# One transformer kernel: the order of half products, exponentials and copies around its attentions

## The reference, cut to what matters

```python
logits = jnp.einsum('bqhd,bkhd->bhqk', qi, k) * scale      # plus a bias
logits = jnp.where(valid, logits, NEG)
p = jax.nn.softmax(logits, axis=-1)
out = jnp.einsum('bhqk,bkhd->bqhd', p, v)
...
wts = jax.nn.softmax(jnp.stack(lses), axis=0)               # dilated: three patterns joined
mixed = jnp.concatenate([o_a, o_b], axis=-1) @ w_out
```

## Time and profile before

| | |
|---|---|
| median of three runs | 1631.53 us (1631.42 to 1632.28) |
| the profiled execution | 1632.0 us, span 1630.3 us, mean granted clock 0.998 |
| PE busy | 1599.5 us, 98% of the span, 9172 matmuls |
| DVE, ACT, POOL busy | 1123.3 us (69%), 942.7 us (58%), 123.8 us (8%) |
| HBM | 281.81 MB read, 174 GB/s over the span |
| costliest lines | L1121 and L1122 (feed-forward, 27% and 13% of the chain that ended last), L836 to L838 (12%, 12%, 11%) |

### The profile page before, as it was taken

One profiled execution on the slowest core, in us unless ns is written; L12 is line 12 of the kernel. 1 busy time (PEld: TensorE's weight loads), 2 busy tenths in 40 slices (PEclk: granted clock), 3 DMA queues, 4 the chain that ended last, 5 costly groups with the idle time before them and its releaser, 6 DMA issues.

```text
span 1630.3 us, 25016 instructions
## 1 busy us (share of the span) xinstructions
PE 1599.5 (98%) x9172; PEld 1367.7 (84%) x9172; DVE 1123.3 (69%) x1788; ACT 942.7 (58%) x1534; POOL 123.8 (8%) x183
## 2 busy tenths in 40 slices
PE   7999999999999999999999899999999999899999
PEld 7887888898788888888888688888888888688887
DVE  5956666787776668766667577667766765677666
ACT  5556555568765556555557565556555565665554
POOL 1612000000000000000003400000000001510000
PEclk9999999999999999999999999999999999999999
DMA  9333464673346553655754046565564674035642
GB/s 337 126 129 104 164 223 157 215 279 130 130 155 213 173 193 131 219 189 197 254 171 156 1 155 202 184 200 187 169 217 163 232 237 171 1 117 195 224 162 102
DMA packets 216790, 283.95 MB, mean 174 GB/s; under 512 B 8329, under 2 KB 152713, under 8 KB 216713
## 3 DMA queue, kind: packets, MB, share of 16 engines
q1 hardware_dynamic: 216330, 282.72, 51.3%
q10 hardware_dynamic: 382, 0.20, 0.0%
HBM read 281.81 MB, written 1.09 MB: 174 GB/s over the span
## 4 chain that ended last, share of the span: by engine, by line
PE 87%; DVE 6%; ACT 3%; POOL 1%; issue 1%; ACTq 0%; DVEq 0%
PE banks L1121 27%; PE banks L1122 13%; PE banks L836 12%; PE banks L837 12%; PE banks L838 11%; PE banks L1486 1%; PE banks L1530 1%; PE banks L1510 1%; PE banks L959 1%; PE banks L1173 1%; PE banks L1880 1%; PE banks L1169 1%; PE banks L761 1%; DVE ring_kept L385 1%; PE banks L1170 1%
## 5 line engine op out<-in xcount | busy, mean ns | idle before, releaser
L1121 PE MATMUL banks<-act_both,ring 128*128 128x512 f32 x1008 | 350.1, 390 | 0.0
L1121 PE MATMUL banks<-act_both,ring_kept 128*128 128x512 f32 x1008 | 350.0, 390 | 0.0
L1122 PE MATMUL banks<-act_both,ring 128*128 128x256 f32 x1008 | 278.5, 276 | 0.0
L1122 PE MATMUL banks<-act_both,ring_kept 128*128 128x256 f32 x1008 | 278.5, 276 | 0.0
L1240 ACT ACTIVATE normed<-banks 128x512 f32<-128x512 f32 x132 | 78.7, 596 | 255.0 <-PE banks L1122 254.9
L1121 PEld LDWEIGHTS banks<-act_both,ring_kept 128*128 128x128 f32 x1008 | 189.2, 188 | 40.1
L1121 PEld LDWEIGHTS banks<-act_both,ring 128*128 128x128 f32 x1008 | 189.2, 188 | 39.8
L836 PE MATMUL banks<-ffn_down_hi,ffn_hidden_both 128*128 128x512 f32 x504 | 197.5, 392 | 0.0
L837 PE MATMUL banks<-ffn_down_lo,ffn_hidden_both 128*128 128x512 f32 x504 | 197.5, 392 | 0.0
L838 PE MATMUL banks<-ffn_down_hi,ffn_hidden_both 128*128 128x512 f32 x504 | 196.0, 389 | 0.0
L1122 PEld LDWEIGHTS banks<-act_both,ring_kept 128*128 128x128 f32 x1008 | 189.2, 188 | 2.2
(11 more groups left out here) (448 smaller groups left out, 2865.6 us busy)
## 6 DMA issues: line engine op xcount, KB each, us to landing
weight_slots<-in_ffn_w SPq DMA_DIRECT2D x44, 1024.0 KB, 7.5
weight_slots<-in_ffn_w_gate SPq DMA_DIRECT2D x44, 1024.0 KB, 5.2
weight_slots<-in_ffn_w_up SPq DMA_DIRECT2D x44, 1024.0 KB, 7.8
weight_slots<-in_ffn_w_down SPq DMA_DIRECT2D x88, 512.0 KB, 8.3
weight_slots<-in_ffn_w SPq DMA_DIRECT2D x44, 512.0 KB, 8.4
weight_slots<-in_ev_w_in SPq DMA_DIRECT2D x6, 2048.0 KB, 14.0
weight_slots<-in_od_w_in SPq DMA_DIRECT2D x5, 2048.0 KB, 10.1
weight_slots<-in_ab_w_in SPq DMA_DIRECT2D x4, 2048.0 KB, 9.0
```

Source lines behind the costliest of these rows:

```text
L1121: pe.matmul(bank, k.hi(n)[:, q, :], k.act_both[:, q], start=q == 0, stop=False, skip_group_check=True)
L1122: return pe.matmul(bank[:, 0:S], k.lo(n)[:, q, :], k.act_hi[:, q, :], start=False, stop=q == KD - 1, skip_group_check=True)
```

## The change

- Even layer and latent attention get `soon_from=5`: from step 5 on, the remainder of a tile (`lower_part`) stands at the end of VectorE's step in which its rounded copy is made, and not at the start of the next step, so ahead of that step's split of weights.
- Wherever a step flips the odd head directly behind the scores or the even flip (`soon`), ScalarE takes the odd copy first, ahead of the rounded copy of the duo before.
- Latent layer: the second half of product part 0 goes from step 6 to the end of step 7, that of part 1 from step 8 into step 9, directly ahead of the first half of part 2, which goes from step 10 to step 9; the second halves of parts 2 and 3 come at the ends of steps 10 and 13. One split of weights goes from step 3 to step 4.
- Dilated attention gets `ahead=(5,)`: in its step 5 (step 9 of the chain) TensorE runs scores, the half parts, then both flips of duo 0; VectorE takes the factors of the first pair in that step, behind its scores' bias pass, and those of the second pair one step later, where they stood two steps later; ScalarE takes the exponentials of two of three duos of the second pair in step 5, those of the third in step 6.
- Sparse layer: the exponentials of duo 0 go from m = 21 to m = 20; the sums, the root, the scaling, the compressed logits, their exponentials and the compressed probabilities each go one step later. TensorE's part of the side chain keeps its steps.

```diff
@@ Attention.tensor
+        if i in self.ahead:
+            scores(i)
+            between()
+            flips(d, 0)
+            flips(d, 1)
+            return
         if d >= 0:
             flips(d, 0)
         if i < self.duos:
             scores(i)
-        soon = d >= 0 and (self.apart(d) or i < self.duos and not parts)
+        soon = self.soon(i, parts)
@@ Attention.vector
         d = self.duo_at(i - 2)
-        if self.closes(d):
+        if self.closes(d) and (self.soon_from is None or i - 1 < self.soon_from):
             lower_part(self.pairs[d // G]["tile"])
         d = self.duo_at(i)
+        if i in self.ahead:
+            add_bias(i)
+            factors(d // G)
+            copy_even(d)
+            return
         if d >= 0:
             copy_even(d)
+        if i - 1 in self.ahead:
+            factors(d // G + 1)
...
-        if G > 1 and d >= 0 and d % G == 0:
+        if G > 1 and d >= 0 and d % G == 0 and not self.ahead:
             factors(d // G)
+        d = self.duo_at(i - 1)
+        if self.soon_from is not None and i >= self.soon_from and self.closes(d):
+            lower_part(self.pairs[d // G]["tile"])
@@ Attention.scalar
+        if self.soon(i, parts):
+            copy_odd(self.duo_at(i))
         d = self.duo_at(i - 1)
         if self.closes(d):
...
             act.activation(k.act_hi[:, self.first_tile + tile], self.mixed(tile), ACT.Copy).then_inc(self.at.act_b.sem, 1)
+        if i in self.ahead:
+            exponentials(i // G, range(0, G - 1))
+        if i - 1 in self.ahead:
+            exponentials(i // G - 1, range(G - 1, G))
         d = self.duo_at(i)
-        if d >= 0:
+        if d >= 0 and not self.soon(i, parts):
             copy_odd(d)
-        if i < self.duos and i % G == G - 1:
+        if i < self.duos and i % G == G - 1 and i not in self.ahead:
             exponentials(i // G)
@@ attend
             def first_halves():
+                for m in (joined_at or {}).get(i, ()):
+                    out.half_part(pe, m, 1)
                 for m in parts:
@@ latent_layer
-        attend(k, block, Chain(mla, dil, 4), out, {6: [0], 8: [1], 10: [2], 12: [3]}, {1: 3, 3: 4, 11: 5, 13: 6, 15: 8},
-               side=ab, tile_waits=tile_waits, fills={1: 6, 2: 5, 3: 4, 4: 4, 5: 8}, fill_free=ab.copied[-2])
+        attend(k, block, Chain(mla, dil, 4), out, {6: [0], 8: [1], 9: [2], 12: [3]}, {1: 3, 4: 4, 11: 5, 13: 6, 15: 8},
+               joined_at={9: [1]}, ends_at={7: [0], 10: [2], 13: [3]}, side=ab, tile_waits=tile_waits, fills={1: 6, 2: 5, 3: 4, 4: 4, 5: 8}, fill_free=ab.copied[-2])
@@ Sparse.scalar
             ins.then_inc(self.key_placed.sem, 1)
+            self.att.scalar(act, 0)
         if m == 21:
             self.square(act, 4, 24, 26)
-            self.att.scalar(act, 0)
+
+    def step_scalar(self, act, i):
+
+        T = self.TILE
+        if i == 1:
             act.wait_ge(*self.summed.after(4))
             x = self.rs[:, :, 24:30]
             self.k.act.done(act, act.activation(x, x, ACT.Ln))
             act.activation(x, x, ACT.Exp, scale=-0.5).then_inc(self.rooted.sem, 1)
...
+        if i == 3:
             act.wait_ge(*self.shifted.after(1))
@@ Sparse.step_vector
+        if i == 1:
             dve.wait_ge(*self.squared.after(5))
             self.sums(dve, 24, 26)
...
-        if i == 1:
+        if i == 2:
             dve.wait_ge(*self.rooted.after(4))
             self.scale_twice(dve, 24, 26, 0)
             self.scale_twice(dve, 28, 30, S).then_inc(self.scaled.sem, 1)
-        if i == 2:
+        if i == 3:
...
-        if i == 3:
+        if i == 4:
             dve.wait_ge(*self.exps.after(1))
...
+        if i == 5:
             k.dve.done(dve, dve.reciprocal(smf, smf))
```

More of the change, by code:

```diff
@@ L1396, in __init__ @@
     def __init__(self, k, ctx, pairs, first_tile, base=None, banks=(4, 5, 6, 7), started=(), values_in=None,
-                 homes=None, alone=True):
-        self.alone = alone
+                 homes=None, alone=True, ahead=(), soon_from=None):
+        self.alone, self.ahead, self.soon_from = alone, ahead, soon_from
         self.k, self.pairs, self.first_tile = k, pairs, first_tile
@@ L1470, in duo_at, with soon @@
         return -1
+    def soon(self, i, parts):
+        d = self.duo_at(i)
+        return d >= 0 and (self.apart(d) or i < self.duos and not parts)
     def tensor(self, pe, i, between=None, parts=()):
@@ L1612, in vector, with scalar, exponentials @@
         d = self.duo_at(i + 1)
-        if G > 1 and d >= 0 and d % G == 0:
+        if G > 1 and d >= 0 and d % G == 0 and not self.ahead:
             factors(d // G)
-    def scalar(self, act, i):
+        d = self.duo_at(i - 1)
+        if self.soon_from is not None and i >= self.soon_from and self.closes(d):
+            lower_part(self.pairs[d // G]["tile"])
+    def scalar(self, act, i, parts=()):
         k, G = self.k, self.G
-        def exponentials(m):
+        def exponentials(m, units=range(G)):
             sink = self.pairs[m].get("sink")
-            if not self.plain(m):
+            if not self.plain(m) and units[0] == 0:
                 act.wait_ge(*self.at.dve_b.after(sum(not self.plain(n) for n in range(m + 1))))
             top = self.nmax[:, m] if G > 1 or sink else self.nmax_u[:, m, :, :, 0]
-            for g in range(G):
+            for g in units:
                 for j in range(2):
@@ L1635, in exponentials @@
                 ins = act.activation(self.esink[:, m], self.esink[:, m], ACT.Exp)
-            ins.then_inc(self.at.probs_ready.sem, 1)
+            if units[-1] == G - 1:
+                ins.then_inc(self.at.probs_ready.sem, 1)
         def copy_odd(d):
@@ L1747, in _ @@
         for i in range(begun, att.steps):
-            att.scalar(act, i)
+            att.scalar(act, i, (parts_at or {}).get(i, ()))
             if side:
@@ L2142, in even_layer @@
                                  for p in range(fox.H // 2)], NH, banks=(6, 7, 4, 5), started=(fox_ready, k.product_copied.after(-3)),
-                        values_in=k.product_copied.after(0))
+                        values_in=k.product_copied.after(0), soon_from=5)
         attend(k, block, att, out, {0: [0], 1: [1], 3: [2], 4: [3], 6: [4], 7: [5]}, {0: 3, 1: 4, 3: 5, 4: 6, 5: 7, 6: 8, 7: 10},
@@ L3009, in vector, with scalar @@
             self.second.vector(dve, i - self.shift)
-    def scalar(self, act, i):
-        self.first.scalar(act, i)
+    def scalar(self, act, i, parts=()):
+        self.first.scalar(act, i, parts)
         if i >= self.shift:
-            self.second.scalar(act, i - self.shift)
+            self.second.scalar(act, i - self.shift, parts)
     def late_tile(self, e):
@@ L3035, in latent_layer @@
                                  for p in range(ab.H // 2)], 0, banks=(4, 5, 6, 7),
-                        started=(ab.head_placed.after(8),), values_in=ab.copied[-1], homes=ab.homes, alone=False)
+                        started=(ab.head_placed.after(8),), values_in=ab.copied[-1], homes=ab.homes, alone=False, soon_from=5)
         product(k, block, "ab_in", KD, pieces, enter, scaled=True, side=ab, then=None)
@@ L3043, in latent_layer @@
                                  for p in range(2)], NH, banks=(4, 5, 6, 7), started=(k.logits_ready.after(0),),
-                        values_in=k.heads_done.after(0), homes=ab.wide_homes)
+                        values_in=k.heads_done.after(0), homes=ab.wide_homes, ahead=(5,))
         out = OutProduct(k, "ab_out", 6)
@@ L3403, in vector @@
             ins.then_inc(self.vblk_made.sem, 1)
[L3404 to L3408, removed]
     def first_vector(self, dve, i):
@@ L3420, in step_vector @@
         if i == 1:
+            dve.wait_ge(*self.squared.after(5))
+            self.sums(dve, 24, 26)
+            self.sums(dve, 28, 30, 128)
+            k.dve.done(dve, dve.memset(self.rs[:, :, 26:28], 1.0))
+            self.add_eps(dve, 24, 30)
+        if i == 2:
             dve.wait_ge(*self.rooted.after(4))
```

5 lines of the change are left out of this document (1 added, 4 removed).

## The result

| | median | ratio to before, 95% interval |
|---|---|---|
| before, runs beside it | 1632.41 us (20 runs) | |
| after | 1635.09 us (1631.82 to 1636.26, 20 runs) | 1.0014 [1.0008, 1.0020] |

The change made the kernel about 2.3 us slower (0.0014 x 1632.4 = 2.3); the forecast was 0.4 us faster. Of the 4.0 us between the forecast of 1631.1 us and the 1635.09 us measured, which lies above the range of 1628.2 to 1634.0, 0.9 us is the kernel before itself, which had a median of 1631.53 us in the runs that the forecast started from and 1632.41 us here. The profiled execution of after took 1635.02 us (span 1633.3 us).

What follows compares the result with a forecast made beforehand. TensorE, busy nearly all the time, was taken as the bound, so only its waits (14.1 us in attention) could give time back. Terms -0.05 - 1.75 + 1.9 - 0.5 = -0.4 us gave 1631.1 us, range 1628.2 to 1634.0.

Steps and rivals of the forecast that it cites:

- 1, even layer: Even layer, last two remainders a step sooner: -0.05 us, bounds -0.15 and +0.2.
- 2 and 3, latent and dilated: Latent values start sooner; dilated half parts cover waits, new waits come: -1.75 us together, bounds -2.3 and -0.9.
- 4, sparse exponentials: Sparse layer: first exponentials sooner, but doubled keys' scaling later, so TensorE waits and its clock falls: +1.9 us.
- 5, odd copies: Sparse step 9: flip no longer waits 0.96 us for ScalarE's odd copy: -0.5 us, bounds -0.95 and 0.
- the forecast 4.6 us: Latent and dilated stretch: waits taken away, 0.95 + 1.30 + 0.67 + 1.28 + 0.4 us, before new waits of 2.8 us.
- from there VectorE, nearly always busy, sets the pace: Sparse layer, from VectorE's copy after the flip behind the doubled keys to the first half part: VectorE sets the time.
- bits of the side chain ... add a little: Sparse layer: side-chain pieces moved behind later waits add a little; no separate size given, within the +1.9 us.
- The bound of +3.3: Upper bound, sparse exponentials: the 1.2 us of side work now late in steps 3 to 5 is on the path in full.
- The lower bound: Sparse exponentials, +0.3 us: at 2.4 GHz throughout, eight flips and the three next take about 1.3 us less.
- elsewhere the copies that change places are hidden behind products or VectorE: Outside sparse step 9, the odd copies' new order was given no gain.
- (d): Rival: the sparse wait is dearer, +3.3 us, 1632.5 us, up to 1635 with split or GpSimd last; chance 0.08.
- (a): Rival: clock falls in the dilated steps, costing 1.7 to 3.5 us, 1632.8 to 1634.6 us; chance 0.16.

Runs made afterwards that it cites:

- latent_only: Kernel before with only the latent layer's part of the change, odd copies' order there included: 1631.06 us, ratio 0.9990 [0.9981, 0.9999].
- sparse_only: Kernel before with only the sparse side-chain part of the change (first exponentials and side chain): 1637.91 us, ratio 1.0036 [1.0022, 1.0049].
- no_sparse: Kernel after with the sparse first exponentials and side chain as before, odd copies' new order kept: 1628.90 us, ratio 0.9983 [0.9974, 0.9992].
- odd_only: Kernel before with only the odd copies' new order in the sparse layer: 1630.51 us, ratio 0.9987 [0.9978, 0.9996].
- after_filled: Kernel after with unread products (15, 5, 6 and 4) ahead of four TensorE waits in the sparse layer: 1630.88 us, ratio 0.9993 [0.9984, 1.0002].
- keys_later: Kernel after with TensorE's flips of the doubled keys moved behind the scores of step 3: 1632.06 us, ratio 1.0002 [0.9993, 1.0011].
- the halves: early_fill and late_fills, each with some of the unread products of after_filled: 1631.69 us (ratio 0.9998) and 1633.11 us (ratio 1.0005).
- early_fill: Kernel after with only the 15 unread products ahead of the doubled keys: 1631.69 us, ratio 0.9998 [0.9989, 1.0007].
- late_fills: Kernel after with only the 5, 6 and 4 unread products in sparse steps 4 and 5: 1633.11 us, ratio 1.0005 [0.9996, 1.0014].
- keys_later_filled: Kernel after, doubled keys' flips behind step 3's scores, unread products ahead of five TensorE waits in steps 2, 3, 5: 1629.25 us, ratio 0.9983 [0.9974, 0.9992].
- no_sparse_filled: no_sparse with eight unread products ahead of the sparse layer's first flip: 1628.88 us, ratio 0.9977 [0.9968, 0.9986] against before.
- before_filled: Kernel before with eight unread products ahead of the sparse layer's first flip: 1631.56 us, ratio 0.9992 [0.9983, 1.0001].

## Why the prediction was wrong

The parts, each against its own steps (us; measured by ratio or, where a stage shows it, by rows):

| part | forecast | measured |
|---|---|---|
| 1, even layer | -0.05 | 0.0 (rows) |
| 2 and 3, latent and dilated | -1.75 (-2.3 to -0.9) | -1.6 (rows, and latent_only) |
| 4, sparse exponentials | +1.9 (+0.3 to +3.3) | +5.8 (rows), +5.9 (sparse_only), +5.1 (after against no_sparse) |
| 5, odd copies | -0.5 (-0.95 to 0) | -1.8 (rows), -2.1 (odd_only) |
| sum | -0.4 | +2.3 |

**Parts 1 to 3 hold.** The last latent values come 20.13 us behind the stage's first scores, where the earlier trace rows had 914.49 - 893.35 = 21.14: -1.0 us (forecast -0.95). The step-8 wait of 1.30 us is gone, the new waits are 0.74, 0.98 and 0.38 us (forecast 0.7, 1.1, 0.5), and the last products are at 942.29 (forecast 942.0). The new waits add up to 2.1 us and not to 2.8, so the waits that went were worth less than the forecast 4.6 us as well; that these errors cancel is luck.

**Part 4 was right up to the flip behind the doubled keys, and wrong behind it.** Counted from the first scores: first exponential 1.38 us sooner (forecast 1.37), first flip 1.36 sooner (1.4), flips of the doubled keys 1.81 later (1.75) behind a wait of 3.64 (3.6), and the flip behind them 14.17 - 12.31 = 1.86 us later (1387.1 against 1385.38: 1.7). The prediction carried these 1.9 us on to the first half part: "from there VectorE, nearly always busy, sets the pace". That is the step that failed, in two terms.

The clock: it was priced once, at about 1.3 us for eight flips and the three next. By the fills it is 3.8 us of the stretch (3.4 us by the ratios). The rows of after_filled put it in two places. At the odd flip of step 5 after is 24.38 - 22.74 = 1.64 us behind after_filled; from there to the first half part, where the clock falls again behind the waits of 1.24 and 1.58 us and within that of 1.21 us, it loses the other 6.85 - 4.68 = 2.17 us: scores, values and the half part run at 1.2 GHz, and VectorE waits for them (0.95 us for the scores at 1401.70). It stays low behind the first half part too; up to the last values the two are 65.07 - 60.60 = 4.5 us apart.

The side work: "bits of the side chain ... add a little" is 0.9 us by the kernel with later flips, beside 1.1 us for the place of the doubled keys in TensorE's queue. At 2.4 GHz throughout the part costs 27.42 - 25.43 = 2.0 us, not 0.3. That after is just 1.87 us behind before at the odd flip of step 5 is in part luck: the new order of the odd copies had won 22.51 - 21.80 = 0.71 us by then, where the prediction had counted on "a little", and against no_sparse after is 2.58 us behind there. The bound of +3.3 had the late side work in full but one fall only, so it did not reach.

Two smaller slips stand in the prediction of this part. The lower bound doesn't follow from its own numbers: 1.9 less the 1.3 us for the clock is +0.6, not +0.3. And TensorE did not stand for 3.6 us with its next flips ready: without the doubled keys in the way keys_later still waits 1.39 us there for GpSimd.

**Part 5 failed at "elsewhere the copies that change places are hidden behind products or VectorE".** Before, TensorE waited 2.5 us for odd copies in steps 4 to 6. Only 1.5 us of that is covered by VectorE. Step 9 itself gave 0.8 us, within its bounds.

**The rivals.** (d), the dearer sparse wait, is nearest to what happened; its 0.08 was too low and its price, +3.3 us, too small. (a) put the risk of the clock in the dilated steps, where the waits are shorter than 1 us; it comes there in one profile of nine, at 1.0 us, and behind two waits that together last 0.74 + 0.97 = 1.71 us, less than the 2.12 us from which the prediction had it decide; the dear place was steps 4 to 6 of the sparse layer, where the prediction expected VectorE "nearly always busy" and did not ask what TensorE's pauses would then do. The two errors of size, +3.9 and -1.3 to -1.6, have opposite signs; the sum missed by 2.7 us.

**What stays open.** Where the clock falls differs between executions of one kernel: after's 20 runs have mean clocks of 0.995 to 0.999 and times of 1631.82 to 1636.26 us, and the two fastest (1631.82 and 1631.84 us) are those at 0.998 and 0.999. No trace of those two exists, so which fall they lack isn't shown. The division of the 3.8 us into 1.64 and 2.17 us holds for two profiled executions. The ratios can't confirm it: the halves take 2.6 and 1.5 us, each a difference of two ratios with intervals of 1.0 and 1.5 us each way, and in the profiles of both halves the fall that was left came at another place than in after. Why one execution has a fall behind a wait and another has none behind the same wait is open.

## What to carry to other kernels

When a supplier is moved one step later, move its consumer on an in-order queue as well, or cost the wait of everything queued behind it, on both engines: here TensorE stood 3.64 us and VectorE 2.70 us for one entry that had kept its step, and moving it was worth 1.1 us at an unchanged clock. Where waits get longer on TensorE, price the lower clock at every pause of the stretch that follows, by the work that runs uncovered behind it, and not once at the longest. A wait that the profile gives to a copy is worth what is left until the next late thing, so look for that one in each step before calling it hidden.

## What the runs showed of the hardware

- The clock fell to 1.2 GHz behind waits far shorter than the 2.12 us of before: 0.74 and 0.97 us in the dilated steps of latent_only, 0.77 us and then 0.98 and 1.59 us in early_fill. The same waits in the dilated steps (0.74 and 0.98 us), and one of 0.76 us at the first flip of the sparse layer, left it at 1.00 in after.
- How long it stayed low differed as well: in the sparse layer from about 1384.0 to 1387.5 in after and from about 1379.8 to 1390.0 in late_fills, which does the same work up to step 4.
- Matmuls that nobody reads, put into waits of the sparse layer behind which the clock had fallen, went with a clock of 1.00 through the stretch in the profiles of after_filled, keys_later_filled, no_sparse_filled and before_filled; in early_fill and late_fills, which had them at some of these waits, it still fell at others. They gained 3.4 us where nothing covered the falls (after), and 1.0 to 1.3 us, not clear of noise, where VectorE did.
- One VectorE pass of 128x240 took 0.41 us with GpSimd idle in before, and 0.77 us (1397.91) in after, beside a GpSimd pass that ran from 1396.51 for 1.90 us; in after_filled it took 0.50 us beside such a pass. So a side step that is moved may get longer by what it then runs beside; no run separates the two.
